# Modulation columns from stationary weights, and the second weight chunk in halves

## The chip, the cores and the metric

The kernel runs on one core of a Trainium2 chip. The metric is the device time of one execution in microseconds. The kernel before takes 1946.04 us, the median of three runs (1945.29 to 1946.46).

## The reference, cut to what matters

The program is one layer of a diffusion backbone over 1024 latent tokens and 256 context tokens, 1024 channels wide. It is written in float32:

```
mod_x = silu(c) @ w_mod + b_mod          # 6 * 1024 columns
mod_c = silu(c_ctx) @ w_mod + b_mod
sh1, sc1, g1, sh2, sc2, g2 = split(mod_x, 6);  csh1, csc1, ... = split(mod_c, 6)
hx = rms_norm(x, g) * (1 + sc1) + sh1
hc = rms_norm(ctx, g) * (1 + csc1) + csh1
fx, qx, kx, vx = split_projection(hx @ w_in)
fc, qc, kc, vc = split_projection(hc @ w_in)
# attention and a 2-D Fourier mixer over them, output projection,
# then a mixture of 16 experts (router, top 128 tokens for each expert) and a last norm
```

For this case only the beginning matters: the first 2048 columns of `silu(c) @ w_mod` and `silu(c_ctx) @ w_mod` (the shift `sh1` and the scale `sc1` for both streams), and the projection `h @ w_in`, whose `h` cannot be formed before shift and scale are known.

## The kernel before, in words

The kernel has three phases, one behind the other: `nc_phase_a` (modulation, norms, the input projection and the Fourier transform's first half), `nc_phase_b` (attention, output projection, router) and `nc_phase_m` (the experts). Each engine runs a list of its own, written out by hand in program order, and semaphores tie the lists together: `x.then_inc(s, 1)` counts up when an instruction is done, `wait_ge(s, n)` holds the engine's list until the count is reached. An engine never goes around a wait.

Float32 products are made in two ways. In the modulation, TensorE (called PE in the profile) multiplies plain float32 operands; each such product of the program shows as two instructions in the trace. In the projection, each operand is split into a rounded high part and a remainder (`w_hi`, `w_lo`, `h_hi`, `h_lo`), and three products hi*hi, hi*lo, lo*hi of 512 columns each replace one.

**Modulation columns.** The first 2048 columns of `w_mod` come as eight units of 256 columns, 1 MB each (L251), unit after unit on SyncE's (SP's) queue into eight slots of SBUF. Five of the units (`ON_PE`: 0, 1, 3, 4, 6) are multiplied by TensorE (L749): the two conditioning columns `c_sig` are the stationary operand (the weights loaded into the array), the unit's 256 columns move through, and the result is two rows of 256 in PSUM. ScalarE (ACT) copies each pair of rows to `c_rows` (L454), and when all five are there ten small transposes turn them into columns (L761). The other three units (`ON_DVE`: 2, 5, 7) are weighed and summed by VectorE (DVE, L575 and L576, 16 instructions a unit), and TensorE sums the result over the partitions by products with a vector of ones (L756), which gives columns at once. When all columns stand in bank 7 of PSUM (`c_col_done`), VectorE makes `mod_col` from them, six small instructions (L634 to L636, `cols_done`).

**The first latent tile.** ScalarE squares and scales the tile's rows (L369, L373; the root is on GpSimd, here POOL, `rstd`, L333 and L335), TensorE turns them (`turn`, L683), and ScalarE applies scale and shift to eight pieces of 128 columns (`turn` in its own list, L383), rounds them to `h_hi` (`high`, L389), and VectorE forms `h_lo` (`low`, L519). `turn(0, 0)` and `turn(0, 1)` are the lower and the upper four pieces.

**The weights.** `w_in` comes in three chunks of 512 columns, 2 MB each, in the order 1, 0, 2 behind the eight units on the same queue (L253). For each half of a chunk ScalarE rounds `w_raw` to `w_hi` (`weights`, L399) and VectorE forms `w_lo` (L515). `w_hi` of chunk 1 lies where units 0 and 1 lay, that of chunk 0 where units 2 and 3 lay; so the rounding also waits until those units are used.

**The projection** (`project`, from L687) then runs over ten tiles on TensorE, for each latent tile chunks 1, 0 and 2 with 24 products each (L699), with the turning of the next tile between them. `project(0, 1)` waits for `h_lo` of tile 0, for both halves of chunk 1 and for the rows' copies. VectorE's list beside it holds the remaining `w_lo`, the next `h_lo`, and the rest of the modulation (`modulation`, rows of `w_mod` through a ring of three buffers, which SP refills).

Of the kernel before, what the change touches and what calls it, by code (L numbers as in the profile page):

```python
# [143 lines left out]
def after(eng, sem_, v):  # L144

    if not (isinstance(v, int) and v <= 0):
        eng.wait_ge(sem_, v)


def nc_phase_a(nc, sem, a, psum, ident, ones, eps_c, ks, vs, x_odd, f_tok, q_d, mod_d, x_d, ctx_d, w_mod, w_in):  # L150
# [3 lines left out]
    def at(name, shape, dt, off):  # L154
# [45 lines left out]
    slot = [at(f"a_slot{i}", [P, KD, UM], F32, o * KB) for i, o in enumerate(slot_at)]  # L200

    s = {n: sem("a_" + n) for n in (
        "ident_done", "small_in", "kv_tab", "rope_in", "vec_t", "silu_done", "c_row_done", "c_col_done", "cols_done", "unit_used",
        "wh_done", "wl_done", "x_in", "ss_done", "mean_done", "rstd_done", "xn_done", "xT_done", "hf_done", "hh_done", "hl_done",
        "pj0", "pj1", "pj2", "ev0", "ev1", "ev2", "sq_done", "v_done", "g_done", "ss16_done", "eps_done", "rstd16_done", "rope_done",
        "qt_done", "qhi_done", "qlo_done", "q_out", "k_out", "mod_used", "row_mm", "row_ev", "row_out", "first_used",
        "dve_order", "pool_order", "wf_zero", "chan_in", "wf_in", "pm_done", "ab_mm", "ab_done", "g_mm", "gt_done", "mid_done", "q0_in")}
# [1 line left out]
    dft_in = [sem(f"f_dft_in{i}") for i in range(4)]  # L209
    unit_in = [sem(f"a_unit_in{i}") for i in range(8)]  # L210
    w_raw_in = [sem(f"a_w_raw_in{i}") for i in range(NCH)]
    ring_in = [sem(f"a_ring_in{i}") for i in range(RING)]
    NC_UNITS, NR_UNITS = 2 * D // UM, 4 * D // UM
    XT, PJ, QT, MB = 0, 2, 5, 7
# [20 lines left out]
    def w_parts(c):  # L235

        return 2 * (1, 0, 2).index(c)

    ON_DVE = (2, 5, 7)
    ON_PE = tuple(u for u in range(NC_UNITS) if u not in ON_DVE)  # L240

    with nc.Block() as block:

        @block.sync
        def _(sp):
# [4 lines left out]
            for u in range(NC_UNITS):  # L250
                sp.dma_start(slot[u][:, :, :].rearrange("p k n -> p (k n)"), w_mod[u]).then_inc(unit_in[u], 16)  # L251
            for c in (1, 0, 2):
                sp.dma_start(w_raw[:, c, :, :].rearrange("p k n -> p (k n)"), w_in[c]).then_inc(w_raw_in[c], 16)  # L253
                if c == 1:
                    sp.dma_start(g_qk[:, 0, :], a["q_norm_g"][0].partition_broadcast(P)).then_inc(s["kv_tab"], 16)
                    sp.dma_start(g_qk[:, 1, :], a["k_norm_g"][0].partition_broadcast(P)).then_inc(s["kv_tab"], 16)
# [61 lines left out]
        def _(pool):  # L318
# [11 lines left out]
            def rstd(n):  # L330
                st = stat[:, n % 2, :]
                pool.wait_ge(s["ss_done"], n + 1)
                pool.tensor_tensor(st[:, 1:2], st[:, 0:1], eps_c[:, 1:2], ALU.add).then_inc(s["mean_done"], 1)  # L333
                pool.wait_ge(s["mean_done"], n + 1)
                pool.tensor_tensor(st[:, 2:3], st[:, 1:2], eps_c[:, 0:1], ALU.pow).then_inc(s["rstd_done"], 1)  # L335
# [12 lines left out]
                pool.tensor_tensor(ss[:, 0, h0:NH], ss[:, 1, h0:NH], ss[:, 2, h0:NH], ALU.pow).then_inc(s["rstd16_done"], 1)  # L348

            rstd(0)  # L350
            rstd(1)
            for n in range(TS + 1):
                if 1 < n + 1 < TS:
# [6 lines left out]
        def _(act):  # L360
            def load_x(n):
                after(act, s["xT_done"], 2 * (n - 1))
                act.dma_start(xbuf(n)[:, :], x_d[n] if lat(n) else ctx_d[n - TL]).then_inc(x_in[n % 2], 16)
# [25 lines left out]
                act.activation(h_hi[n % 2][:, :, :], h_f[n % 2][:, :, :], ACT.Copy).then_inc(s["hh_done"], 1)  # L389

            def weights(c, half):
                act.wait_ge(w_raw_in[c], 16)
                if c == 1:
                    act.wait_ge(s["unit_used"], 2)
                elif c == 0:
                    act.wait_ge(s["unit_used"], 3)
                    act.wait_ge(s["first_used"], 1)
                k = slice(4 * half, 4 * half + 4)
                act.activation(w_hi[:, c, k, :], w_raw[:, c, k, :], ACT.Copy).then_inc(s["wh_done"], 1)  # L399

# [48 lines left out]
                           psum[:, 6, 0:2 * KD].rearrange("p (j k) -> p j k", k=KD), ACT.Silu).then_inc(s["silu_done"], 1)  # L449
            square(0)  # L450
            normal(0)
            for i, u in enumerate(ON_PE):
                act.wait_ge(s["unit_used"], i + 1)
                act.activation(c_rows[:, i * UM:(i + 1) * UM], psum[0:2, 2 + i % 2, 0:UM], ACT.Copy).then_inc(s["c_row_done"], 1)  # L454
                if i == 1:
                    load_x(2)
            weights(1, 0)
            weights(1, 1)
            turn(0, 0)
            turn(0, 1)  # L460
            high(0)
            square(1)
            normal(1)
# [36 lines left out]
        def _(dve):  # L500
# [130 lines left out]
            dve.wait_ge(s["c_col_done"], 1)  # L631
            cols = psum[:, 7, 0:4 * KD].rearrange("p (m k j) -> p m j k", k=KD, j=2)
            for j in range(2):
                dve.tensor_tensor(mod_col[:, 1, j, :], cols[:, 0, j, :], bg_col[:, 0:KD], ALU.add)  # L634
                link(dve.tensor_tensor(mod_col[:, 0, j, :], cols[:, 1, j, :], bg_col[:, KD:2 * KD], ALU.add))
                dve.scalar_tensor_tensor(out=mod_col[:, 0, j, :], in0=mod_col[:, 0, j, :], scalar=1.0,  # L636
                                         in1=g_col, op0=ALU.add, op1=ALU.mult).then_inc(s["cols_done"], 1)
            weights(1, 0)
            weights(1, 1)
            low(0)  # L640
            weights(0, 0)
# [31 lines left out]
        def _(pe):  # L673
# [12 lines left out]
            def project(n, c, part=range(KD)):  # L686
                if c == 2 and not lat(n) or c == 1:  # L687
                    pe.wait_ge(s["hl_done"], n + 1)
                if n == TS - 1:
                    pe.wait_ge(s["ev1"], TL)  # L690
                else:
                    after(pe, s[("ev0", "ev1", "v_done")[c]], n)
                if n == 0:
                    pe.wait_ge(s["wl_done"], w_parts(c) + 2)
                    if c == 1:
                        pe.wait_ge(s["c_row_done"], len(ON_PE))
                for k in part:
                    for x_, w_ in ((h_hi, w_hi), (h_hi, w_lo), (h_lo, w_hi)):
# [43 lines left out]
            for i, u in enumerate(ON_PE):  # L742
                if i == 1:
                    turn(0, 0)
                    turn(0, 1)
                pe.wait_ge(unit_in[u], 16)
                after(pe, s["c_row_done"], i - 1)
                for k in range(KD):
                    m = pe.matmul(psum[0:2, 2 + i % 2, 0:UM], c_sig[:, k, :], slot[u][:, k, :], start=(k == 0), stop=(k == KD - 1))  # L749
                m.then_inc(s["unit_used"], 1)  # L750
            for i, u in enumerate(ON_DVE):
                pe.wait_ge(s["first_used"], i + 1)
                for h in range(2):
                    for j in range(2):
                        b = 2 * u + h
                        pe.matmul(psum[:, 7, 2 * b + j:2 * b + j + 1], first_acc[i][:, j, h * P:(h + 1) * P], ones[:, 0:1], start=True, stop=True)  # L756
            pe.wait_ge(s["c_row_done"], len(ON_PE))
            for i, u in enumerate(ON_PE):
                for h in range(2):
                    b = 2 * u + h  # L760
                    m = pe.transpose(psum[:, 7, 2 * b:2 * b + 2], c_rows[:, (2 * i + h) * P:(2 * i + h + 1) * P], ident[0:2, 0:2])  # L761
            m.then_inc(s["c_col_done"], 1)
            for n in range(TS):
                if n == TL:
                    project(n, 2, range(KD // 4))
# [986 lines left out]
```

## Time and profile before

| | before |
|---|---|
| median of three runs | 1946.04 us |
| the profiled execution | 1948.3 us |
| its span, first to last instruction | 1946.5 us |
| PE busy | 1808.8 us (93%) |
| DVE busy | 1571.8 us (81%) |
| ACT busy | 1287.0 us (66%) |
| POOL busy | 352.1 us (18%) |
| mean granted TensorE clock | 0.974 |

The profile is that of one execution. Its times are counted from the first instruction. PE is busy nearly throughout; the modulation and the first projection lie in the first 58 us. PEld is TensorE's loading of stationary operands, which overlaps with its products. The granted clock is a share of TensorE's full 2.4 GHz, so 0.50 is 1.2 GHz.

### The profile page before, as it was taken

What the parts mean: (1) busy time and instruction counts of PE and PEld (TensorE: products, weight loads), DVE (VectorE), ACT (ScalarE), POOL (GpSimd) and SP (SyncE); (2) the same over time, 40 slices, a digit from 0 to 9 for tenths busy, and PEclk for the clock granted to TensorE, in tenths of its full rate; (3) what the DMA queues carried; (4) which work ended last, traced back from release to release, by engine and by line L of the source; (5) the groups of instructions that cost most, each with busy time, mean ns of one, the idle gap of its engine ahead of it and who ended that gap; (6) DMA issues with size and microseconds to landing.
All of it is one profiled execution on the core that took longest, in us unless ns stands there. A gap on an engine that the chain in (4) does not pass through costs nothing.

```text
span 1946.5 us, 27774 instructions
## 1 busy us (share of the span) xinstructions
PE 1808.8 (93%) x8627; PEld 1440.4 (74%) x8627; DVE 1571.8 (81%) x1944; ACT 1287.0 (66%) x1905; POOL 352.1 (18%) x319
## 2 busy tenths in 40 slices
PE   6999988999999997189999999999999999999995
PEld 3777766777777775178888888888888888888884
DVE  5888676777777774769998899999889989988986
ACT  3454375776677764167777777777777777777774
POOL 0333342222122222411011011101001100110113
PEclk8999999999999999589999999999999999999998
DMA  9465671221122201669999999999999999999996
GB/s 379 145 190 160 166 207 36 64 67 52 47 64 63 63 25 37 237 240 405 391 385 369 405 387 377 394 389 381 368 401 388 376 381 402 381 368 404 378 376 247
DMA packets 115204, 515.48 MB, mean 265 GB/s; under 512 B 17185, under 2 KB 43209, under 8 KB 64465
## 3 DMA queue, kind: packets, MB, share of 16 engines
q1 hardware_dynamic: 108960, 492.30, 67.6%
q0 software_dynamic: 4752, 17.30, 3.4%
q10 hardware_dynamic: 1440, 5.24, 0.7%
q8 instruction: 26, 0.43, 0.1%
q14 instruction: 26, 0.20, 0.0%
HBM read 484.86 MB, written 27.33 MB: 263 GB/s over the span
## 4 chain that ended last, share of the span: by engine, by line
PE 56%; DVE 2%; DMA 0%; POOL 0%; issue 0%; ACT 0%; DVEq 0%; ACTq 0%; POOLq 0%
PE banks L1688 36%; PE banks L1713 18%; PE banks L1700 1%; PE banks L1669 1%; DVE topi L1550 1%; DVE top L1548 1%; DVE cand L1551 1%; DVE raw L1643 0%; DMA xe<-h_scratch,icol 0%; POOL fst L1469 0%; DMA out<-raw 0%; ACT banks L1539 0%; DVE ysc L1610 0%; DVE ysc L1650 0%; POOL out L1473 0%
## 5 line engine op out<-in xcount | busy, mean ns | idle before, releaser
L1582 DVE TENSOR_TENSOR w_lo<-raw,w_hi 128x2048 fp32r<-128x2048 f32 x252 | 565.9, 2287 | 72.0 <-ACT w_hi L1491 72.0
L1491 ACT ACTIVATE w_hi<-raw 128x2048 fp32r<-128x2048 f32 x256 | 470.5, 1918 | 10.0 <-DMA raw<-in_w_exp 9.9
L1688 PE MATMUL banks<-w_hi,x_hi 128*128 128x512 f32 x1024 | 405.6, 396 | 1.4 <-DVE x_lo L1576 1.4
L1688 PE MATMUL banks<-w_hi,x_lo 128*128 128x512 f32 x1024 | 400.1, 391 | 0.0
L1688 PE MATMUL banks<-w_lo,x_hi 128*128 128x512 f32 x1024 | 399.7, 390 | 0.0
L1590 DVE TENSOR_TENSOR d_lo<-raw,d_hi 128x1024 fp32r<-128x1024 f32 x256 | 296.3, 1220 | 1.5 <-ACT d_hi L1513 1.4
L1513 ACT ACTIVATE d_hi<-raw 128x1024 fp32r<-128x1024 f32 x256 | 258.2, 1061 | 33.7 <-DMA raw<-in_w_exp 20.4
L1068 ACT ACTIVATE pth<-banks 128x384 fp32r<-128x384 f32 x320 | 157.2, 491 | 125.6 <-PE banks L1255 122.2
L1133 DVE TENSOR_TENSOR ptl<-banks,pth 128x384 fp32r<-128x384 f32 x320 | 177.7, 555 | 76.8 <-ACT pth L1068 72.0
L1688 PEld LDWEIGHTS banks<-w_hi,x_lo 128*128 128x128 f32 x1024 | 192.8, 188 | 40.8
L1688 PEld LDWEIGHTS banks<-w_hi,x_hi 128*128 128x128 f32 x1024 | 193.0, 188 | 39.7 <-DVE x_lo L1576 1.8
L1688 PEld LDWEIGHTS banks<-w_lo,x_hi 128*128 128x128 f32 x1024 | 193.1, 189 | 38.1
L1125 DVE TENSOR_REDUCE mn<-banks 128x1 f32<-128x512 f32 (+1 forms) x288 | 171.4, 595 | 56.4 <-PE banks L1238 55.8
L1422 POOL TENSOR_TENSOR carry<-carry 128x1 f32<-128x1 f32 x32 | 44.6, 1394 | 915.7 <-DVE ysc L1610 583.5
L1497 ACT ACTIVATE sil<-banks 128x512 f32<-128x512 f32 x64 | 38.2, 597 | 257.3 <-PE banks L1688 257.3
L1052 ACT ACTIVATE pr<-banks,mn 128x512 f32<-128x512 f32 (+1 forms) x288 | 176.6, 614 | 7.7 <-DVE mn L1129 7.2
L1255 PE MATMUL banks<-ident,pr 128*128 128x128 f32 x960 | 158.9, 275 | 10.8 <-DVE ptl L1133 9.0
L1237 PE MATMUL banks<-ks,qt 128*128 128x512 f32 (+1 forms) x288 | 144.3, 501 | 17.4 <-ACT pr L1052 15.9
L1713 PE MATMUL banks<-d_hi,h_hi 128*128 128x512 f32 x512 | 157.9, 390 | 2.6 <-DVE h_lo L1596 2.6
L1713 PE MATMUL banks<-d_hi,h_lo 128*128 128x512 f32 x512 | 157.7, 389 | 0.0
L1713 PE MATMUL banks<-d_lo,h_hi 128*128 128x512 f32 x512 | 157.7, 389 | 0.0
L1255 PEld LDWEIGHTS banks<-ident,pr 128*128 128x128 f32 x960 | 118.8, 140 | 46.3 <-DVE ptl L1133 16.8
(217 smaller groups left out, 2721.4 us busy)
## 6 DMA issues: line engine op xcount, KB each, us to landing
raw<-in_w_exp SPq DMA_DIRECT2D x384, 1024.0 KB, 7.7
a_ring<-in_w_mod SPq DMA_DIRECT2D x32, 512.0 KB, 7.3
qt<-q_scratch SPq DMA_DIRECT2D x64, 192.0 KB, 4.4
a_slot<-in_w_mod SPq DMA_DIRECT2D x8, 1024.0 KB, 13.9
a_w_raw<-in_w_in SPq DMA_DIRECT2D x3, 2048.0 KB, 28.7
q_scratch<-a_qst SPq DMA_DIRECT2D x16, 384.0 KB, 4.4
xr<-in_x SPq DMA_DIRECT2D x8, 512.0 KB, 5.1
acc_scratch<-x SPq DMA_DIRECT2D x8, 512.0 KB, 3.7
```

Source lines behind the costliest of these rows:

```text
L1052: act.activation(pr[(h // 3 % 2) * 3 + h % 3][:, lo:hi], psum[:, (NCH * h + c) % 4, 0:hi - lo], ACT.Exp, bias=mn[:, h, 3:4], scale=-1.0, a ...
L1068: act.activation(pth[:, k % 4, :], psum[:, PTB + k % 2, 0:REP * P], ACT.Copy).then_inc(s["hi_done"], 1)
L1125: ins = dve.tensor_reduce(mn[:, i, c:c + 1], psum[:, (NCH * i + c) % 4, 0:hi - lo], AX, ALU.min)
L1133: dve.tensor_tensor(ptl[:, k % 4, :], psum[:, PTB + k % 2, 0:REP * P], pth[:, k % 4, :].bitcast(F32), ALU.subtract).then_inc(s["lo_done"], 1)
L1237: pe.matmul(o, qt[:, i, 0, :], ks[:, i // 3, lo:hi], start=True, stop=False)
L1255: ins = pe.transpose(psum[:, PTB + k % 2, r * P:(r + 1) * P], pr[(g % 2) * 3 + r][:, kt * P:(kt + 1) * P], ident[:, :])
L1491: act.activation(w_hi[which][c][:, :], raw[which][c][:, :], ACT.Copy).then_inc(s["hi_done"], 1)
L1513: act.activation(d_hi[k][:, :], raw[2][k // 2][:, k % 2 * D:(k % 2 + 1) * D], ACT.Copy).then_inc(s["d_hi_done"], 1)
L1582: dve.tensor_tensor(w_lo[which][c][:, :], raw[which][c][:, :], w_hi[which][c][:, :].bitcast(F32), ALU.subtract).then_inc(s["lo_done"], 1)
L1590: dve.tensor_tensor(d_lo[k][:, :], raw[2][k // 2][:, k % 2 * D:(k % 2 + 1) * D], d_hi[k][:, :].bitcast(F32), ALU.subtract).then_inc(s["d_l ...
L1688: i = pe.matmul(psum[:, 2 * (j % 2) + which, :], x_[par][:, k, :], w_, start=(k == 0 and w_ is hi and x_ is x_hi), stop=(k == KD - 1 and x ...
L1713: i = pe.matmul(psum[:, Y + h, :], x_[:, k, :], w_[k][:, h * 512:(h + 1) * 512], start=(j == 0 and k == 0 and x_ is h_hi and w_ is d_hi), ...
```

## The change

The units on TensorE become 0, 2, 3, 5 and 7, those on VectorE 1, 4 and 6. For a unit on TensorE the weights are now the stationary operand: for each half of 128 columns and each of eight pieces of the contraction, 128 x 128 of the unit are loaded and the two columns of `c_sig` move through; the result is two columns in bank 7. The rows, their copies and their transposes are gone. The order on TensorE is otherwise kept: unit 0, the turning of tile 0, the other units, the products with ones.

Chunk 1 of `w_in` comes in two transfers, and ScalarE rounds its lower half when the first has landed. `w_lo` of the lower half goes to GpSimd, between `rstd(0)` and `rstd(1)`; VectorE makes only the upper half. The upper half of tile 0's scale and shift (`turn(0, 1)`) goes from ScalarE to VectorE, ahead of its `weights(1, 1)`. `project(0, .)` waits for the halves of `w_lo` one by one. Between the columns and `project(0, 1)` TensorE runs 14 products of 512 columns into a bank that `project(0, 1)` overwrites; they wait for the first half of `w_hi`.

```diff
-    ON_DVE = (2, 5, 7)
+    ON_DVE = (1, 4, 6)
 # SP
-                sp.dma_start(w_raw[:, c, :, :].rearrange("p k n -> p (k n)"), w_in[c]).then_inc(w_raw_in[c], 16)
+                if c == 1:
+                    for half in range(2):
+                        sp.dma_start(w_raw[:, c, 4 * half:4 * half + 4, :].rearrange("p k n -> p (k n)"),
+                                     w_in[c][:, 4 * half * UC:(4 * half + 4) * UC]).then_inc(w_raw_in[c] if half else w_half_in, 16)
+                else:
+                    sp.dma_start(w_raw[:, c, :, :].rearrange("p k n -> p (k n)"), w_in[c]).then_inc(w_raw_in[c], 16)
 # GpSimd
             rstd(0)
+            pool.wait_ge(s["rstd_done"], 1)
+            pool.wait_ge(s["wh_done"], 1)
+            pool.tensor_tensor(w_lo[:, 1, 0:4, :], w_raw[:, 1, 0:4, :], w_hi[:, 1, 0:4, :].bitcast(F32), ALU.subtract).then_inc(s["wl0_done"], 1)
+            pool.wait_ge(s["wl0_done"], 1)
             rstd(1)
 # ScalarE
             def weights(c, half):
-                act.wait_ge(w_raw_in[c], 16)
+                act.wait_ge(w_half_in if c == 1 and half == 0 else w_raw_in[c], 16)
                 if c == 1:
-                    act.wait_ge(s["unit_used"], 2)
+                    act.wait_ge(s["unit_used"], 1)
+                    act.wait_ge(s["first_used"], 1)
...
-            for i, u in enumerate(ON_PE):
-                act.wait_ge(s["unit_used"], i + 1)
-                act.activation(c_rows[:, i * UM:(i + 1) * UM], psum[0:2, 2 + i % 2, 0:UM], ACT.Copy).then_inc(s["c_row_done"], 1)
-                if i == 1:
-                    load_x(2)
+            load_x(2)
             weights(1, 0)
             weights(1, 1)
             turn(0, 0)
-            turn(0, 1)
             high(0)
 # VectorE
-            weights(1, 0)
+            dve.wait_ge(s["xT_done"], 2)
+            dve.wait_ge(s["cols_done"], 2)
+            for k in range(4, 8):
+                ins = dve.tensor_scalar(h_f[0][:, k, :], psum[:, XT + 1, k % 4 * P:(k % 4 + 1) * P],
+                                        mod_col[:, 0, 0, k:k + 1], mod_col[:, 1, 0, k:k + 1], ALU.mult, ALU.add)
+            ins.then_inc(s["hf_done"], 1)
             weights(1, 1)
             low(0)
 # TensorE
-                after(pe, s["c_row_done"], i - 1)
-                for k in range(KD):
-                    m = pe.matmul(psum[0:2, 2 + i % 2, 0:UM], c_sig[:, k, :], slot[u][:, k, :], start=(k == 0), stop=(k == KD - 1))
+                for h in range(2):
+                    b = 2 * u + h
+                    for k in range(KD):
+                        m = pe.matmul(psum[:, 7, 2 * b:2 * b + 2], slot[u][:, k, h * P:(h + 1) * P], c_sig[:, k, :], start=(k == 0), stop=(k == KD - 1))
...
-            pe.wait_ge(s["c_row_done"], len(ON_PE))
-            for i, u in enumerate(ON_PE):
-                for h in range(2):
-                    b = 2 * u + h
-                    m = pe.transpose(psum[:, 7, 2 * b:2 * b + 2], c_rows[:, (2 * i + h) * P:(2 * i + h + 1) * P], ident[0:2, 0:2])
-            m.then_inc(s["c_col_done"], 1)
+            pe.wait_ge(s["wh_done"], 1)
+            for i in range(14):
+                pe.matmul(psum[:, PJ + 1, :], w_hi[:, 1, 0, 0:P], w_hi[:, 1, 0, :], start=True, stop=True)
```

## Rows read from the trace of the kernel before

**Rows 1.** The page's chain that ended last, shares by engine and line:

```profile
PE 56%; DVE 2%; DMA 0%; POOL 0%; issue 0%; ACT 0%; DVEq 0%; ACTq 0%; POOLq 0%
```

**Rows 2.** Stretches: length, busy and count of PE, PEld, DVE, ACT, POOL; clock; DMA:

```profile
31.70:33.90 2.20, 0.00 (x0) 0.00 (x0) 2.20 (x6) 0.26 (x1) 0.00 (x0) 0.98 0.96 382
37.00:43.40 6.40, 0.00 (x0) 0.00 (x0) 6.26 (x9) 5.35 (x12) 0.39 (x1) 0.50 0.98 413
43.40:47.40 4.00, 3.99 (x9) 3.14 (x10) 0.35 (x1) 3.33 (x3) 0.55 (x2) 0.50 1.00 373
47.50:50.90 3.40, 3.40 (x17) 2.77 (x16) 3.40 (x2) 3.40 (x3) 0.00 (x0) 1.00 0.07 28
```

**Rows 3.** Waits of PE from 40 to 260 us: total, times, longest:

```profile
PE banks L712 <- DVE a_qkn L560: 6.4, 7, 1.3
```

**Rows 4.** Timeline to 52 us: start, busy, instruction, idle before and its releaser:

```profile
9.20 5.64 PE L749 MATMUL banks<-a_slot,a_c_sig 128*2 128x256 f32 x16 [2.95 <-DMA a_slot<-in_w_mod]
14.66 5.63 DVE L576 SCALAR_TENSOR_TENSOR a_first<-a_slot,a_c_sig,a_first 128x256 f32<-128x256 f32 x14
15.80 13.97 PE L749 MATMUL banks<-a_slot,a_c_sig 128*2 128x256 f32 x64
21.50 0.62 DVE L575 TENSOR_SCALAR a_first<-a_slot,a_c_sig 128x256 f32<-128x256 f32 x2 [1.22 <-DMA a_slot<-in_w_mod]
29.71 1.95 PE L756 MATMUL banks<-ones,a_first 128*128 128x1 f32 x16
33.65 3.71 ACT L399 ACTIVATE a_w_hi<-a_w_raw 128x2048 fp32r<-128x2048 f32 x2 [3.46 <-DMA a_w_raw<-in_w_in]
33.96 1.87 PE L756 MATMUL banks<-ones,a_first 128*128 128x1 f32 x8 [2.31 <-DVE a_first L576]
37.02 0.17 DVE L634 TENSOR_TENSOR a_mod_col<-banks,a_bg_col 128x8 f32<-128x8 f32 x1 [3.12 <-PE banks L761]
37.73 4.49 DVE L515 TENSOR_TENSOR a_w_lo<-a_w_raw,a_w_hi 128x2048 fp32r<-128x2048 f32 x2
37.91 2.90 ACT L383 ACTIVATE a_h_f<-banks,a_mod_col 128x128 f32<-128x128 f32 x8 [0.56 <-DVE a_mod_col L636]
40.84 1.06 ACT L389 ACTIVATE a_h_hi<-a_h_f 128x1024 fp32r<-128x1024 f32 x1
42.14 1.22 DVE L519 TENSOR_TENSOR a_h_lo<-a_h_f,a_h_hi 128x1024 fp32r<-128x1024 f32 x1
43.41 0.79 PE L699 MATMUL banks<-a_w_hi,a_h_hi 128*128 128x512 f32 x1 [6.42 <-DVE a_h_lo L519]
51.60 0.19 PEld L699 LDWEIGHTS banks<-a_w_hi,a_h_hi 128*128 128x128 f32 x1 [0.38 <-DVE a_w_lo L515]
```

**Rows 5.** The eight units' transfers: issues with first and last start, time to landing:

```profile
L251 SPq DMA_DIRECT2D a_slot<-in_w_mod x8: 360/440/738, 2.2 to 6.3; - x8
DMA to landing us min/median/max: 6.8/13.9/21.4
```

**Rows 6.** The timeline's operations nearest to those that the change adds:

```profile
64.05 4.01 POOL L341 TENSOR_TENSOR a_sq<-a_prj 128x1024 f32<-128x1024 f32 x1 [1.55 <-ACT vs L420]
84.15 2.74 POOL L341 TENSOR_TENSOR a_sq<-a_prj 128x1024 f32<-128x1024 f32 x1 [1.01 <-DVE a_qkn L560]
105.60 0.42 DVE L523 TENSOR_TENSOR vs<-banks,vs 128x256 fp32r<-128x256 f32 x1
```

**Rows 7.** GpSimd's own subtractions of this shape, ns min/median/max:

```profile
L1411 POOL TENSOR_TENSOR w_lo<-raw,w_hi x4: 4524/4526/4537, 797.7 to 811.2; 128x2048 fp32r<-128x2048 f32 x4
```

**Rows 8.** Later stretches of TensorE at the low clock, columns as in the stretches above:

```profile
303.47:306.88 3.41, 3.41 (x14) 2.95 (x13) 1.14 (x3) 0.95 (x3) 0.00 (x0) 0.50 0.00 0
306.90:309.00 2.10, 2.10 (x11) 1.49 (x10) 1.42 (x4) 0.97 (x4) 0.00 (x0) 1.00 0.04 1
781.31:784.72 3.41, 2.67 (x13) 2.68 (x14) 0.00 (x0) 0.62 (x2) 0.68 (x1) 0.50 0.38 154
```

**Rows 9.** The timeline's products of the router, sixteen columns moving:

```profile
782.95 3.43 PE L1221 MATMUL banks<-wrt,h2t 128*128 128x16 f32 x16
```

More of the change, by code:

```diff
@@ L202, in nc_phase_a @@
     s = {n: sem("a_" + n) for n in (
-        "ident_done", "small_in", "kv_tab", "rope_in", "vec_t", "silu_done", "c_row_done", "c_col_done", "cols_done", "unit_used",
-        "wh_done", "wl_done", "x_in", "ss_done", "mean_done", "rstd_done", "xn_done", "xT_done", "hf_done", "hh_done", "hl_done",
+        "ident_done", "small_in", "kv_tab", "rope_in", "vec_t", "silu_done", "c_col_done", "cols_done", "unit_used",
+        "wh_done", "wl_done", "wl0_done", "x_in", "ss_done", "mean_done", "rstd_done", "xn_done", "xT_done", "hf_done", "hh_done", "hl_done",
         "pj0", "pj1", "pj2", "ev0", "ev1", "ev2", "sq_done", "v_done", "g_done", "ss16_done", "eps_done", "rstd16_done", "rope_done",
@@ L211, in nc_phase_a @@
     w_raw_in = [sem(f"a_w_raw_in{i}") for i in range(NCH)]
+    w_half_in = sem("a_w_half_in")
     ring_in = [sem(f"a_ring_in{i}") for i in range(RING)]
@@ L391, in weights @@
             def weights(c, half):
-                act.wait_ge(w_raw_in[c], 16)
+                act.wait_ge(w_half_in if c == 1 and half == 0 else w_raw_in[c], 16)
                 if c == 1:
-                    act.wait_ge(s["unit_used"], 2)
+                    act.wait_ge(s["unit_used"], 1)
+                    act.wait_ge(s["first_used"], 1)
                 elif c == 0:
                     act.wait_ge(s["unit_used"], 3)
-                    act.wait_ge(s["first_used"], 1)
                 k = slice(4 * half, 4 * half + 4)
@@ L630, in _ @@
                 first_unit(i, u)
-            dve.wait_ge(s["c_col_done"], 1)
+            dve.wait_ge(s["c_col_done"], len(ON_DVE))
             cols = psum[:, 7, 0:4 * KD].rearrange("p (m k j) -> p m j k", k=KD, j=2)
@@ L692, in project @@
                     after(pe, s[("ev0", "ev1", "v_done")[c]], n)
-                if n == 0:
-                    pe.wait_ge(s["wl_done"], w_parts(c) + 2)
-                    if c == 1:
-                        pe.wait_ge(s["c_row_done"], len(ON_PE))
                 for k in part:
+                    if n == 0 and k % 4 == 0:
+                        if c == 1 and k == 0:
+                            pe.wait_ge(s["wl0_done"], 1)
+                        else:
+                            pe.wait_ge(s["wl_done"], w_parts(c) + k // 4)
                     for x_, w_ in ((h_hi, w_hi), (h_hi, w_lo), (h_lo, w_hi)):
@@ L755, in _ @@
                         b = 2 * u + h
-                        pe.matmul(psum[:, 7, 2 * b + j:2 * b + j + 1], first_acc[i][:, j, h * P:(h + 1) * P], ones[:, 0:1], start=True, stop=True)
-            pe.wait_ge(s["c_row_done"], len(ON_PE))
-            for i, u in enumerate(ON_PE):
-                for h in range(2):
-                    b = 2 * u + h
-                    m = pe.transpose(psum[:, 7, 2 * b:2 * b + 2], c_rows[:, (2 * i + h) * P:(2 * i + h + 1) * P], ident[0:2, 0:2])
-            m.then_inc(s["c_col_done"], 1)
+                        m = pe.matmul(psum[:, 7, 2 * b + j:2 * b + j + 1], first_acc[i][:, j, h * P:(h + 1) * P], ones[:, 0:1], start=True, stop=True)
+                m.then_inc(s["c_col_done"], 1)
+            pe.wait_ge(s["wh_done"], 1)
+            for i in range(14):
+                pe.matmul(psum[:, PJ + 1, :], w_hi[:, 1, 0, 0:P], w_hi[:, 1, 0, :], start=True, stop=True)
             for n in range(TS):
```

## The prediction

> **What bounds the kernel now.** I read the page's chain first: TensorE holds 56% of the span in the chain that ended last [rows 1], and everything behind the first projection hangs on TensorE's order. So the question is by how much the first projection moves, and whether what follows moves with it. The stretches come next: between 37.0 and 43.4 us TensorE does nothing, while VectorE (6.26 us) and ScalarE (5.35 us) are nearly full [rows 2]. The timeline says what it waits for [rows 4]. `project(0, 1)` starts at 43.41, released by `h_lo`. Backwards: `h_lo` 1.22 us from 42.14, held up by the two `w_lo` (4.49 us from 37.73); `h_hi` 1.06; eight pieces of scale and shift 2.90 from 37.91; the columns, whose first small instruction starts at 37.02 and whose six take 0.8 us; before them the products with ones (1.87 us from 33.96), released by VectorE's third unit, and the ten transposes. In parallel the weights land, 33.65, and ScalarE rounds both halves until 37.4. So two arms meet: columns and weights. Last, the projection runs low at first: nine products in 4.0 us at a granted clock of 0.50 (1.2 GHz), then some fifteen whole ones in 3.4 us at 1.00 (2.4 GHz), 0.44 against 0.227 us each [rows 2]. That costs 9 x 0.21 = 1.9 us.
>
> **The weights' arm.** The last unit has landed by 6.3 + 21.4 = 27.7 us [rows 5], chunk 1 by 33.65. Halfway between is 30.7: there the first half lands. ScalarE rounds it until 32.6 (half of 3.71 is 1.86), then, waiting for the second, until 35.5 [rows 4]. The extra issue on SP costs nothing as long as the queue is ahead of the transfers (the units were all issued by 6.3 us). `load_x(2)` is issued on ScalarE some 3 us earlier, no longer behind two copies; its 0.5 MB shares the transfers with the units and delays some of them by up to 0.5/1 of the 2.46 us that a 1 MB unit takes ((21.50 - 9.20)/5), 1.2 us, but not chunk 1, as the bytes ahead of that are the same.
>
> GpSimd's half of `w_lo`: no such operation stands in this stage, but the same shape later takes 4.52 to 4.54 us [rows 7]. So 32.6 + 4.5 = 37.1. A square on GpSimd takes 4.01 us in one place and 2.74 in another [rows 6]; with that ratio it would be 6.6 us, ready at 39.2. I take 4.5, a row of the operation itself; either end is before `h_lo` (below), so it costs nothing. Behind it in GpSimd's list waits `rstd(1)`, for which `normal(1)` and behind it the remaining roundings wait on ScalarE; ScalarE reaches `square(1)` only at 38.1, so with 4.5 us nobody waits, with 6.6 us 1 us is lost there, which the 5.4 us of `project(0, 1)` mostly cover.
>
> **The columns' arm on VectorE.** One unit takes 0.62 + 5.63 = 6.2 us [rows 4]. Units 1, 4 and 6 land at about 11.7, 19 to 20 and 24 to 25. So it ends at 17.9, 26 and 32.3 (33.9 before).
>
> **The columns' arm on TensorE** is the disputed term. A unit was 8 products, 16 in the trace; 64 of them took 13.97 us, 3.5 us a unit at the high level [rows 4]. Now it is 16 products, 32 in the trace, each with a load of 128 x 128 and two columns. The nearest row is the products with ones, same load and one column: 16 in 1.95 us, 0.122 each, and, when the clock was down, 8 in 1.87, 0.234 each [rows 4]. So a unit costs 3.9 us at the high level or 7.5 at the low one, against 3.5 before; the change pays here and wins only the copies and the ten transposes (1.2 us).
>
> Which level? Before, 16 products of 5.64 us and those behind them at 0.218 say that the first ten or so ran at the low pace, for 4.3 us. If the new stream lifts the clock as fast: 18 instructions in 4.3 us, the other 14 in 1.7, unit 0 done at 15.2; turning 1.0; then nothing waits but unit 7, with 3.9 us each: 20.1, 24.0, 27.9, 31.8. All 24 products with ones then take 2.9, the last eight behind VectorE's 32.3: columns at 34.7, `mod_col` at 35.5 instead of 37.8. That is just when ScalarE has rounded the weights.
>
> For the high level: a stretch of 3.41 us in which loads filled 2.95 us ended with the clock up [rows 8]; the units make TensorE busy without a gap for 22 us, and each long unbroken stretch here ends at the high level. Against: 2.67 busy us of transposes and 16-column products [rows 8, 9] did not lift it, though not all of that stretch was busy; and it had dropped to 0.98 on average by 33.9, only 2.2 us after the narrow products ended [rows 2]. The router's sixteen then ran evenly at 0.214 each. The Trainium skill ("TensorE: Matmul & The Clock Gate", Part 4: PE-mode transpose) says that transposes don't count as busy for the clock in the way other products do; carried over to this stream, TensorE would stay at 1.2 GHz. The trace has a mixed stretch that rose and a narrow one that didn't, so it leaves this open; by that rule the sum is that of rival B. I give the high level the better chance, 2 in 3.
>
> **From there to the projection.** ScalarE: four pieces 1.45 us from 35.5 (half of 2.90), `h_hi` 1.06, at 38.1. VectorE: its four pieces from 35.5. Such a piece from PSUM on VectorE is not in the trace; a PSUM operand of 256 columns takes 0.42 [rows 6], so at most 0.42, at least half of it, 0.21; I take 0.25 (near the width), 1.0 in all: 36.5. `w_lo`'s upper half 2.25 (half of 4.49): 38.75. `h_lo` 1.22: 40.0. The projection starts at 40.0 rather than 43.4: **-3.4 us** (-3.0 if the pieces cost 0.42 and the columns come 0.2 late, -4.0 if VectorE is free by the time `h_hi` is). Nothing behind VectorE's new wait is hurt: its list holds only `w_lo` and `h_lo`, which need the same columns.
>
> The 14 wide products start at 34.7 and end by 37.9 at the high pace, by 40.9 at the low one. They add no result. If the clock outlasts the 2.1 us to 40.0, the 1.9 us of the slow start are gone; if not, they are paid again. I take three quarters: **-1.5 us** (0 to -1.9).
>
> `project(0, 0)` waited 0.38 us for `w_lo` [rows 4]. ScalarE gets to chunk 0 some 3.5 us earlier and VectorE as well, so I count that wait as nearly gone: **-0.3** (0 to -0.4). In sum -5.2 us. From then on TensorE is short of nothing but VectorE's rotated queries, 6.4 us in 7 waits [rows 3], and these follow TensorE's own products. So the shift reaches the end.
>
> The profiled execution took 1948.3 us, its span 1946.5; the sum of differences goes against the median of the runs, 1946.04: **1940.8 us**.
>
> **Rivals.** A (the forecast), chance 0.58: 1939.0 to 1943.0, from the ends above (-7 to -3).
>
> B, slower, 0.32: the clock stays at 1.2 GHz while weights are stationary. Five units at 7.5 us and eight transposes at twice the pace (2.0): 9.2 + 37.5 + 2.0 = 48.7; products with ones 24 x 0.234 = 5.6: columns at 54.3 (with the router's 0.214 a unit is 6.8 and they stand at 50). Then the wide products, up to 14 x 0.44 = 6, now on the path, less once the clock rises: start at 55.5 to 60 instead of 43.4, less 1.9 for a warm start and 0.4: +10 to +14, **1958 us**. It decides as soon as the columns come later than about 40 us, a mean of some 4.6 us a unit. For it speak the router's products and the drop at 33.9, against it the stretch that rose.
>
> C, no change, 0.10: VectorE is nearly as late as TensorE in each tile [rows 3], and if its part is paced by the ring's transfers rather than by TensorE, the start is given back there over eight tiles: all but 1 us, 1945. Against it speaks that no single wait is above 1.3 us.
>
> **How the numbers follow.** About 0.2% (3.9 us) is what a measurement of this kernel can tell from no change. A falls beyond it in 4 of 5 cases: faster 0.46. Same: 0.12 of A and 0.10 of C, 0.22. Slower: B, 0.32. The time is A's. As A and C hold less than 8 in 10 with their edges, the range reaches over B's middle: 1939 to 1959; A's own is 1939 to 1943.
>
> **What would show it.** In the changed profile: the pace of the new unit products, 0.12 us (A) or 0.21 to 0.23 (B), and the granted clock at 35 us; the first small column instruction at about 34.7; the first rounding at 30.7; GpSimd's subtraction of 4.5 us done at 37; the projection's start at 40.0 and whether its first nine products take 2 or 4 us; PE's waits for rotated queries still near 6.4 us. The prediction is wrong if the columns are later than 38, or if the projection starts by 41 and the end doesn't move by 3.

## The result, and the profile after

The changed kernel takes 1962.40 us, the median of six runs (1959.92 to 1964.22), against 1946.29 for the kernel before in the same comparison: a ratio of 1.0075, 95% interval 1.0060 to 1.0089 (the two medians alone would give 1.0083). It is slower, and its time lies above the range I gave. The profiled execution took 1963.47 us with a span of 1961.7, 15.2 us more than before.

The chain of the page looks as it did [rows 1]:

```profile
PE 55%; DVE 2%; DMA 0%; POOL 0%; issue 0%; ACT 0%; DVEq 0%; ACTq 0%; POOLq 0%
```

TensorE's order carries the span as before, so a later start of the projection can move the end. The timeline of the changed kernel, with the columns of [rows 4]:

```profile
9.53 6.96 PE L761 MATMUL banks<-a_c_sig,a_slot 128*128 128x2 f32 x32 [3.27 <-DMA a_slot<-in_w_mod]
18.10 27.30 PE L761 MATMUL banks<-a_c_sig,a_slot 128*128 128x2 f32 x128
31.19 1.91 ACT L409 ACTIVATE a_w_hi<-a_w_raw 128x2048 fp32r<-128x2048 f32 x1 [21.49 <-DMA a_w_raw<-in_w_in]
33.25 4.53 POOL L359 TENSOR_TENSOR a_w_lo<-a_w_raw,a_w_hi 128x2048 fp32r<-128x2048 f32 x1 [24.73 <-ACT a_w_hi L409]
45.26 5.26 PE L768 MATMUL banks<-ones,a_first 128*128 128x1 f32 x24
50.38 5.90 PE L773 MATMUL banks<-a_w_hi 128*128 128x512 f32 x14
50.56 0.17 DVE L639 TENSOR_TENSOR a_mod_col<-banks,a_bg_col 128x8 f32<-128x8 f32 x1 [18.92 <-PE banks L768]
51.46 1.37 DVE L646 TENSOR_SCALAR a_h_f<-banks,a_mod_col 128x128 f32<-128x128 f32 x4
56.21 0.50 PE L710 MATMUL banks<-a_w_hi,a_h_hi 128*128 128x512 f32 x1
62.21 0.50 PE L710 MATMUL banks<-a_w_hi,a_h_hi 128*128 128x512 f32 x1
```

The units on TensorE (L761) take 6.96 us for 32 instructions and 27.30 for 128: 0.213 to 0.218 us each, the pace that I had read as the low level's (0.21 to 0.23), from the first to the last. VectorE waits 18.92 us for the columns. The columns stand at 50.56 instead of 37.02, `project(0, 1)` starts at 56.21 instead of 43.41 (+12.8), and since it runs at full pace from its first product, `project(0, 0)` starts 10.6 us late (62.21 against 51.60). Where the units are meant, "a product" below is one such instruction of the trace; two of them make one product of the program.

The remaining 4.6 us of the 15.2 come in the tiles. PE's waits there and VectorE's, from 50 to 260 us, and VectorE's in the kernel before, from 40 to 260 us, columns as in [rows 3]:

```profile
PE banks L723 <- DVE a_qkn L565: 8.1, 6, 2.2
DVE a_acc L581 <- DMA a_ring<-in_w_mod: 27.8, 8, 5.6
```

```profile
DVE a_acc L576 <- DMA a_ring<-in_w_mod: 26.6, 7, 4.7
```

TensorE waits 8.1 us for rotated queries instead of 6.4, and behind two of these waits, at 158 and at 223 us, its granted clock falls to 0.50 for some 3.4 us, which in the kernel before it doesn't do in the tiles. In this stretch (columns as in [rows 2]) the clock is 0.66 on average:

```profile
157.00:162.00 5.00, 4.71 (x18) 3.76 (x18) 5.00 (x10) 1.16 (x2) 2.75 (x1) 0.66 0.07 16
```

### The profile page after: what moved, and what is told of

It is laid out like the page before. It is cut to its first block, busy times and chain, and to the rows that moved or that the text cites. A ratio compares the mean times of both kernels' runs of the same rounds, so it can differ in the third digit from the quotient of the medians.

```text
span 1961.7 us, 27938 instructions
## 1 busy us (share of the span) xinstructions
PE 1830.7 (93%) x8711; PEld 1473.4 (75%) x8711; DVE 1571.2 (80%) x1947; ACT 1284.3 (65%) x1896; POOL 370.8 (19%) x320
## 4 chain that ended last, share of the span: by engine, by line
PE 55%; DVE 2%; DMA 0%; POOL 0%; issue 0%; ACT 0%; DVEq 0%; ACTq 0%; POOLq 0%
PE banks L1699 36%; PE banks L1724 17%; PE banks L1711 1%; PE banks L1680 1%; DVE topi L1561 1%; DVE top L1559 1%; DVE cand L1562 1%; DVE raw L1654 0%; DMA xe<-h_scratch,icol 0%; POOL fst L1480 0%; DMA out<-raw 0%; ACT banks L1550 0%; POOL fst L1478 0%; DVE ysc L1621 0%; DVE ysc L1661 0%
## 5 line engine op out<-in xcount | busy, mean ns | idle before, releaser
L1433 POOL TENSOR_TENSOR carry<-carry 128x1 f32<-128x1 f32 x32 | 68.5, 2140 | 905.8 <-DVE ysc L1621 583.6
L1136 DVE TENSOR_REDUCE mn<-banks 128x1 f32<-128x512 f32 (+1 forms) x288 | 171.5, 596 | 56.1 <-PE banks L1249 55.6
L1508 ACT ACTIVATE sil<-banks 128x512 f32<-128x512 f32 x64 | 38.4, 599 | 265.1 <-PE banks L1699 265.1
```

The source lines that it names most:

```text
L1136: ins = dve.tensor_reduce(mn[:, i, c:c + 1], psum[:, (NCH * i + c) % 4, 0:hi - lo], AX, ALU.min)
```

## The experiments

Unless said otherwise, an edit is made to the changed kernel; "..." stands for code left out. The ratios are to the kernel before, which had medians of 1947.85, 1947.48 and 1947.25 us in the three comparisons.

### Is it the two moving columns?

Each product moves 128 columns, the two of `c_sig` repeated 64 times:

```diff
-    m = pe.matmul(psum[:, 7, 2 * b:2 * b + 2], slot[u][:, k, h * P:(h + 1) * P], c_sig[:, k, :], ...)
+    m = pe.matmul(psum[:, 7, 2 * b:2 * b + P], slot[u][:, k, h * P:(h + 1) * P],
+                  c_sig[:, k, :].unsqueeze(1).broadcast_to([P, P // 2, 2]), ...)
```

> The changed kernel with one edit: each unit product moves 128 columns (the two conditioning columns, repeated 64 times) past the same stationary weights; the 126 extra columns land on places of the bank that later products overwrite. Theory 1: the clock stayed at 1.2 GHz because almost nothing moved through the array while weights were loaded. Then this stream lifts it some 4 us in: the pace falls from 0.213 to 0.12 to 0.14 us, columns at 34 to 36 us instead of 50.6, the first projection at 40, the time about 1941 us, as rival A and the forecast had it. Theory 2: the loads are slow in this stage for another reason (transfers into SBUF and VectorE's reads beside them), whatever the clock. Then the pace stays at 0.21, and the time at 1960 to 1964 us or more.

1950.67 us, ratio 1.0010 (1.0001 to 1.0019). Its timeline:

```profile
8.86 6.17 PE L761 MATMUL banks<-a_c_sig,a_slot 128*128 128x128 f32 x32 [2.37 <-DMA a_slot<-in_w_mod]
15.74 10.88 PE L761 MATMUL banks<-a_c_sig,a_slot 128*128 128x128 f32 x96
33.17 4.57 POOL L359 TENSOR_TENSOR a_w_lo<-a_w_raw,a_w_hi 128x2048 fp32r<-128x2048 f32 x1 [24.43 <-ACT a_w_hi L409]
35.10 0.17 DVE L639 TENSOR_TENSOR a_mod_col<-banks,a_bg_col 128x8 f32<-128x8 f32 x1 [2.80 <-PE banks L768]
35.38 2.39 DVE L641 SCALAR_TENSOR_TENSOR a_mod_col<-a_mod_col,a_bg_col 128x8 f32<-128x8 f32 x1
42.99 0.79 PE L710 MATMUL banks<-a_w_hi,a_h_hi 128*128 128x512 f32 x1 [4.60 <-DVE a_h_lo L524]
```

With 64 times the moving columns a product takes 0.113 us (10.88 / 96) instead of 0.213, and the columns stand at 35.10, where I had forecast 34.7. So the number of moving columns made the columns late; that it did so by the clock, the next run shows. But the win that I forecast behind it doesn't come. L641, an instruction of 8 columns that takes 0.17 us elsewhere, takes 2.39 and ends at 37.77, when GpSimd's subtraction ends (33.17 + 4.57 = 37.74); I call this the hold. And the 14 wide products are done by 38.4, TensorE has nothing for 4.6 us, and the projection's first products run at a granted clock of 0.50 again.

### Does the narrow stream hold a clock that is up?

Twenty products of the identity run ahead of unit 0, and their results aren't used:

```diff
+            for i in range(10):
+                pe.matmul(psum[:, 5, 0:P], ident[:, :], ident[:, :], start=True, stop=True)
             pe.wait_ge(s["small_in"], 16 * 4)
             pe.transpose(psum[:, 6, 0:5 * KD], vec[:, :], ident[0:5 * KD, 0:5 * KD]).then_inc(s["vec_t"], 1)
+            for i in range(10):
+                pe.matmul(psum[:, 5, 0:P], ident[:, :], ident[:, :], start=True, stop=True)
             pe.wait_ge(s["silu_done"], 1)
```

> The changed kernel with 20 products of 128 columns (identity by identity, results unused) ahead of unit 0, so that the clock can be up when the unit stream begins. Theory 1: the first unit products run at 0.12 us, and some microseconds later the pace falls back to 0.213 for the rest of the stream, because the stream does not hold the clock; columns at about 46 to 49 us. Theory 2: 0.21 from the first product on. Theory 3 (the stream only lacks a start: it holds the clock once it is up): 0.12 throughout, columns near 34.

1962.82 us, one run. Its units in the timeline, and two stretches of them:

```profile
9.42 3.63 PE L765 MATMUL banks<-a_c_sig,a_slot 128*128 128x2 f32 x32
13.98 27.09 PE L765 MATMUL banks<-a_c_sig,a_slot 128*128 128x2 f32 x128
```

```profile
9.40:13.00 3.60, 3.60 (x35) 3.60 (x34) 1.45 (x5) 0.75 (x1) 0.00 (x0) 1.00 1.01 426
16.00:41.00 25.00, 25.00 (x119) 25.00 (x119) 13.93 (x37) 3.82 (x2) 4.52 (x1) 0.50 1.02 423
```

Warmed, unit 0 runs at 0.113 us a product and a clock of 1.00; with the engine still busy without a gap the clock then falls, and units 2 to 7 run at 0.50 for 25 us. So this stream of weight loads with two columns neither lifted the clock (in the changed kernel) nor held it (here), though TensorE's busy share is 100%. The columns stand at 46.22 and the projection starts at 52.09, 4.1 us earlier than in the changed kernel; this one run is no faster, as its tiles take 22.06 us each and those of the changed kernel 21.13 (measured as in the loop below).

### What is the rest of the change worth?

This run has the old units (`c_sig` stationary, rows, copies, transposes, VectorE on 2, 5 and 7) with all the rest of the change:

```diff
-    ON_DVE = (1, 4, 6)
+    ON_DVE = (2, 5, 7)
...
-                for h in range(2):
-                    b = 2 * u + h
-                    for k in range(KD):
-                        m = pe.matmul(psum[:, 7, 2 * b:2 * b + 2], slot[u][:, k, h * P:(h + 1) * P], c_sig[:, k, :], ...)
+                for k in range(KD):
+                    m = pe.matmul(psum[0:2, 2 + i % 2, 0:UM], c_sig[:, k, :], slot[u][:, k, :], ...)
```

> The changed kernel with the units computed as before the change (two rows of 256, copies, ten transposes, VectorE's units 2, 5 and 7), all other parts kept: the halves of chunk 1, GpSimd's share, VectorE's four pieces, the 14 wide products. It tells what these parts are worth by themselves. Theory 1 (all the loss is in the units): faster than before, columns at 37 as before, first projection at about 42.5 and at full clock: 1943 to 1945 us. If GpSimd's share or the second transfer were part of the loss, it would be above 1947 us.

1946.24 us, ratio 0.9993 (0.9983 to 1.0004): no gain that can be told, where I had expected 1943 to 1945. The hold is there as well:

```profile
33.60 4.54 POOL L359 TENSOR_TENSOR a_w_lo<-a_w_raw,a_w_hi 128x2048 fp32r<-128x2048 f32 x1 [24.73 <-ACT a_w_hi L409]
35.70 2.46 DVE L645 SCALAR_TENSOR_TENSOR a_mod_col<-a_mod_col,a_bg_col 128x8 f32<-128x8 f32 x1
43.38 0.50 PE L714 MATMUL banks<-a_w_hi,a_h_hi 128*128 128x512 f32 x1 [3.00 <-DVE a_h_lo L528]
```

The columns stand at 35.4, but VectorE's first small instruction with both operands in SBUF takes 2.46 us, until GpSimd is done at 38.14, and the projection starts where it did before, at 43.38. The Trainium skill ("GPSIMD Engine Reference", section 8, Key points) says that GpSimd shares its SBUF interfaces with VectorE and that instructions with two SBUF inputs contend there; both traces agree, and put the price at 2.2 to 2.3 us for one small instruction.

The changed kernel without the 14 wide products:

```diff
-            for i in range(14):
-                pe.matmul(psum[:, PJ + 1, :], w_hi[:, 1, 0, 0:P], w_hi[:, 1, 0, :], start=True, stop=True)
```

> The changed kernel without the 14 wide products. If they held up the first projection, it starts earlier than 56.2 by up to 4 us and the time falls below 1960. If they only ran beside the scale, the shift and the remainder, the projection still starts at about 56.2, but its first nine or so products run at 0.43 instead of 0.23: 1 to 2 us slower than the changed kernel, about 1964 us.

1963.56 us, ratio 1.0079 (1.0066 to 1.0092). `project(0, 1)` starts at 56.17, as with the wide products, and its first 13 products take 0.43 us each, up to 61.9. So the wide products lie beside VectorE's work and save some 2.5 us at the start; the end shows 1.2 us of it, less than the medians tell apart.

### Without GpSimd's share

This is the kernel with 128 moving columns, in which VectorE makes the low half of `w_lo` itself, ahead of its wait for the columns:

```diff
-            pool.tensor_tensor(w_lo[:, 1, 0:4, :], w_raw[:, 1, 0:4, :], w_hi[:, 1, 0:4, :].bitcast(F32), ALU.subtract)...
+            weights(1, 0)          # VectorE
             dve.wait_ge(s["c_col_done"], len(ON_DVE))
```

> The wide-moving kernel (unit products with 128 moving columns) with GpSimd's subtraction given back to VectorE, which makes the low half of the first weight piece itself ahead of its wait for the columns. Theory 'hold': GpSimd's 4.57 us subtraction held VectorE's small instruction on the scale column (2.39 us for 0.17) until it ended; without it that instruction takes 0.17 us, the columns stand by 37, h_lo is made by 41 and the first projection starts at 41.0 (42.99 with the share). The cost of the move is VectorE's 2.3 us, mostly beside the wait for the columns: at most 0.6 us. Rival 'VectorE's own': the 2.39 us came from something else (a queue, a semaphore, the operand itself), stays, and the first projection starts at 43 or later, since VectorE now has 2.3 us more to do. Time by the first theory 1945 to 1949, by the rival 1951 or more.

With 26 wide products in place of 14:

> The same, with 26 wide products in place of 14 after the columns, so that TensorE is busy until the first projection (12 more at 0.21 us each, 2.6 us: from 38.4 to 41.0). Theory 'idle gap': the fall of the clock at 41.9 in the wide-moving kernel came from TensorE's 4.6 us without work behind the 14 products; with the gap filled, the first 11 products of the projection take 0.21 and not 0.43 us, and project(0, 0) ends at 47 to 48 (51.26 with the gap, 51.6 before the change). Rival: the clock falls for another reason (the load of the stretch before), and the first products are slow all the same; then 50 or later. Time 1942 to 1946 by the first if the tiles keep the lead, 1947 to 1950 by the rival. A third outcome, project(0, 0) early and the end not, says that the tiles give the lead back.

With 22, and `low(0)` ahead of `weights(1, 1)` on VectorE:

> As the one with 26 wide products, with 22, and VectorE makes h_lo ahead of the low half 4 to 7 of the weights, which the first projection needs only 12 products in. h_lo then waits for ScalarE's high part (39.0) alone and stands at 40.2: the first projection starts at 40.3 instead of 41.0, 0.7 us earlier, and the low half is there at 42.5, before the 13th product at 42.9. Rival: the order doesn't matter, because ScalarE's high part is later than I take it to be. Time: 0.7 us under the kernel with 26, within what can be told apart only if the tiles keep the lead.

The old units, VectorE making the low half:

> The kernel with the old units (the modulation vector moving over the weights... that is, stationary) and the rest of the change, with GpSimd's subtraction given back to VectorE as well: what the change is worth without both of its costly parts. Theory 'hold': VectorE's instruction on the scale column takes 0.17 and not 2.46 us, and the first projection starts at 41 (43.38 with the share, 43.41 before the change); the time is 1 to 2 us under the 1946.2 of the kernel with the share if the tiles keep the lead, and no change if they give it back. Rival 'VectorE's own': 2.46 us stay, start 43.4 or later.

| kernel | us | ratio | `project(0, 1)` starts |
|---|---|---|---|
| 128 columns, no share of GpSimd | 1947.06 | 0.9994 (0.9985 to 1.0003) | 41.20 |
| the same, 26 wide products | 1948.18 | 0.9996 (0.9985 to 1.0008) | 44.21 |
| 22 wide products, `h_lo` first | 1948.85 | 1.0004 (0.9996 to 1.0013) | 41.07 |
| old units, no share of GpSimd | 1944.58 | 0.9983 (0.9973 to 0.9994) | 43.03 |

The hold is gone in all four; in the first one's timeline the instruction of 2.39 us is back at 0.17, and the projection starts at 41.2, at full pace:

```profile
35.53 0.17 DVE L638 SCALAR_TENSOR_TENSOR a_mod_col<-a_mod_col,a_bg_col 128x8 f32<-128x8 f32 x1
41.20 0.39 PE L704 MATMUL banks<-a_w_hi,a_h_hi 128*128 128x512 f32 x1
```

That also removes the reason for more wide products: here the clock had fallen to 0.50 by 35, during the products with ones (one moving column), and was up again by 41.2 behind 14 of them. 26 of them, half at the low pace, last until 44.4 and push the projection back: a miss. So is the order of `h_lo`: there the 22 products, not `h_lo`, end at 41.1. The old units' start is a miss by 2 us: VectorE's third unit was done at 34.4 and not 33.6, and the last products and transposes behind it took longer, so that the columns came at 37.4.

The main miss is the time. The first and third kernel have 4.6 and 4.2 us of lead at tile 0 (GpSimd's first square at 59.49 and 59.88; 64.05 before, [rows 6]) and, by the medians, nothing at the end. The profiled execution of the first, 1951.96 us, is its slowest; that of the third, 1946.32, is one of its fastest and still has 2.9 us of the lead at tile 7. Where does the lead go?

### The loop in the tiles

One turn in the trace of the changed kernel (SPq is SP's issuing of transfers):

```profile
136.83 1.29 DVE L572 TENSOR_TENSOR a_qst<-banks,a_qst 128x512 fp32r<-128x512 f32 x2
138.15 3.50 SPq L282 DMA_DIRECT2D ks<-a_qst  x4
141.70 1.29 SPq L285 DMA_DIRECT2D q_scratch<-a_qst  x2
143.03 9.62 SPq L272 DMA_DIRECT2D a_ring<-in_w_mod  x4
150.59 1.67 DVE L581 SCALAR_TENSOR_TENSOR a_acc<-a_ring,a_c_sig,a_acc 128x256 f32<-128x256 f32 x4 [5.56 <-DMA a_ring<-in_w_mod]
156.01 1.22 DVE L565 TENSOR_TENSOR a_qkn<-a_qkn,a_sq 128x1024 f32<-128x1024 f32 x1
```

The split queries (136.83) are stored by six transfers, the load of the modulation's next quarter is issued behind them (143.03), VectorE waits 5.56 us for it, then rotates (156.01), and TensorE's next queries wait for that: a closed loop through SP's queue. A turn takes 20.67 us on average in the kernel before and 20.9 to 22 in those without GpSimd's share. The move:

```diff
-                if n >= 2:
-                    store(n - 2)
                 if n < TL:
                     load(4 * n + 3)
+                if n >= 2:
+                    store(n - 2)
```

It was made in the kernel before, in the changed kernel, in the one with the old units and no share of GpSimd, and in the one with 22 wide products:

> The kernel before the change with one thing moved: in each tile's turn on the transfer queue, the load of the fourth quarter of the modulation rows is issued ahead of the stores of the queries and keys of two tiles earlier, not behind them. It tests why a lead at the start of the tiles isn't kept. Theory 'loop': each tile turns in a loop (queries on TensorE, their split on VectorE, six stores on the transfer queue, then the quarter's load, its landing 7 us later, VectorE's 4 to 5 us wait for it, rotation, next queries), as long as TensorE's own work or longer, so that TensorE waits 0.5 to 1.3 us per tile (6.4 us in all) and the kernel gains what the loop loses: the stores take 4 us of issue (148.45 to 152.7), the quarter before is used by 151.1, so the load goes out 1.7 to 2 us earlier, TensorE's waits for the rotated queries fall to near nothing, and phase A ends 5 to 8 us earlier: 1939 to 1943. Rival 'TensorE-bound': the waits are slack that comes back elsewhere, time within 2 us of before.

> The changed kernel with the same move. It asks where the 4.6 us come from that the changed kernel loses in the tiles beside the 10.6 us it loses ahead of them. Theory 'loop': they are longer turns of the loop (waits of 8.1 us for rotated queries and two stretches of low clock behind them); with the load ahead of the stores both kernels lose the waits, and the difference to the kernel before with the same move is 10 to 12 us, not 16. Rival: the 4.6 us belong to the change itself (for instance x rows or stores arriving in another order), and the difference stays at 15 to 17 us.

> The kernel with the old units and VectorE making its own low half (1944.6), with the same move: its first projection leads by the 0.4 us start and full pace, 2.6 us at the first tile's squares. By 'loop' it keeps that lead and wins 5 to 8 us more: 1936 to 1941, under the kernel before with the move by 2 to 3. By 'TensorE-bound' it stays at 1943 to 1946.

> The kernel with units of 128 moving columns, 22 wide products and h_lo first (1948.8, although its first tile's squares lead by 4.2 us), with the same move. By 'loop' the lead of 4.2 us is kept and the time is 1 to 2 us under the kernel with the old units and the same move: 1935 to 1940. By a rival 'warm units' the 128 moving columns cost something later that no view names yet, and it stays 2 us or more above the kernel with the old units.

The time of a tile is the distance between GpSimd's squares of the tiles 1 and 7, by 6:

| kernel | us | ratio | a tile without the move | with it |
|---|---|---|---|---|
| before | 1938.36 | 0.9954 (0.9936 to 0.9972) | 20.67 | 19.34 |
| changed | 1951.91 | 1.0018 (1.0006 to 1.0030) | 21.13 | 19.34 |
| old units, no share of GpSimd | 1934.90 | 0.9931 (0.9912 to 0.9950) | 20.94 | 19.34 |
| 22 wide products, `h_lo` first | 1938.83 | 0.9949 (0.9931 to 0.9968) | 20.88 | 19.34 |

In the kernel before with the move, SP issues the load ahead of the stores, VectorE waits 0.27 us for it, and TensorE waits once for rotated queries, where it waited seven times [rows 3]; timeline, then PE's and VectorE's waits from 40 to 260 us, then a stretch of 100 us in the tiles, first in the kernel before and then with the move:

```profile
148.58 0.37 SPq L266 DMA_DIRECT2D a_ring<-in_w_mod  x1
149.01 2.58 SPq L276 DMA_DIRECT2D ks<-a_qst  x4
153.12 1.67 DVE L576 SCALAR_TENSOR_TENSOR a_acc<-a_ring,a_c_sig,a_acc 128x256 f32<-128x256 f32 x4 [0.27 <-DMA a_ring<-in_w_mod]
```

```profile
PE banks L712 <- DVE a_qkn L560: 0.5, 1, 0.5
DVE a_acc L576 <- DMA a_ring<-in_w_mod: 2.2, 6, 0.7
```

```profile
100.00:200.00 100.00, 94.82 (x435) 73.03 (x434) 78.82 (x136) 44.37 (x94) 38.57 (x25) 1.00 0.63 174
```

```profile
100.00:200.00 100.00, 100.00 (x466) 77.89 (x464) 83.62 (x142) 48.58 (x105) 38.19 (x27) 1.00 0.69 196
```

All four now take the same 19.34 us a tile, and TensorE, busy for 94.82 of 100 us before, is busy for all 100: it sets the pace, and a lead or a lag at tile 0 is kept through the tiles. Against the kernel before with the move, the one with the old units leads by 3.3 us at the first square and by 3.2 at tile 7, the last one by 3.8 at both. The changed kernel is behind by 9.65 us at the first square (73.93 against 64.28) and by 10.29 at tile 7 (210.65 against 200.36). The two profiled executions differ by 11.0 us (1952.25 and 1941.22); the medians by 13.5, more than the 10 to 12 expected and less than the rival's 15. So the loop made most of the 4.6 us by the profiled executions (15.2 us became 11.0), and about half by the medians (16.1 became 13.5). Where the 2 us between the medians lie is not shown. A candidate is the wait for the output weights, of which more below: 5.9 us in the changed kernel with the move, 3.4 in the kernel before with it.

The last kernel is a miss: 1938.83, where I expected it under the one with the old units, which has 1934.90; the number is that of the rival "warm units". At the end of the tiles they are 1 us apart. Then TensorE waits for the output weights, which GpSimd scales in attention's beginning; the waits of the old units' kernel and of the last one, there:

```profile
289.53 1.13 PE L1217 MATMUL banks<-wout,mix 128*128 128x512 f32 x2 [0.46 <-POOL wout L1035]
```

```profile
292.55 2.07 PE L1209 MATMUL banks<-wout,mix 128*128 128x512 f32 x2 [5.58 <-POOL wout L1027]
```

5.58 against 0.46 us: ahead of that chain GpSimd waited 17.9 us for a transfer (the gain of the later norm) rather than 15.2. Why the transfer came later was not tried. It lands 12.0 to 12.6 us after its issue in six of the fourteen traces and 14.5 to 15.6 in eight. The kernel before, which has no unit of 128 columns, is among the late ones (15.0), but so are all five kernels that have them, so the rival isn't ruled out.

The kernel with the old units, without GpSimd's share and with the load ahead of the stores, at 1934.90 us, is the fastest measured here.

## Why the prediction was wrong

**The failed step is the columns' arm on TensorE**, "I give the high level the better chance, 2 in 3". It was the low pace throughout: 0.213 us a product, some 7 us a unit, where I had bounded it by 7.5 and taken 3.9. I weighed an unbroken busy stretch [rows 8] as what lifts the clock; the narrow kernel is busy without a gap for 27 us and stays low, the warmed one falls while busy, and 128 moving columns alone restore 0.113. The rows of the router [rows 9], sixteen columns and no rise, were the nearer ones in kind: few columns behind a full weight load. The Trainium skill ("TensorE: Matmul & The Clock Gate", Part 4: PE-mode transpose) says of transposes that they don't count as busy for the clock as other products do; carried over to this stream it gave rival B's sum. The trace agrees in effect, with 0.213 us a product throughout; no run shows that the reason is the same as for transposes.

**Rival B's mechanism held**: the units at the router's pace put the columns at 50 (measured 50.56) and the start at 55.5 to 60 (56.21). Its time, 1958, missed 1962.4 by the tiles' part.

**The step "So the shift reaches the end" failed as well.** I read TensorE's 6.4 us of waits [rows 3] as following its own products. They follow a loop over SP's queue, which was my rival C; its mechanism is real, for with 128 moving columns a lead of 4.2 to 4.6 us is gone in the medians, and the tiles shorten to 19.34 us once the load goes first. A lag does reach the end, and grew from 10.6 to 15.2 us on the way. So forecast A would not have reached 1940.8 even with a stream at full pace: the kernels that come nearest to it have 1947.06 to 1948.85.

**GpSimd's half "costs nothing"** was right for the time at which it is done (37.78, forecast 37.1) and wrong in the forecast's own case: with the columns at 35 it holds VectorE until then, and the start is 43.0 to 43.4, not 40.0. In the changed kernel it is done 12.8 us before the columns, and costs nothing there. I had also read the two squares of [rows 6] as one instruction at two speeds; the last section has what they show.

**Right by their rows:** the first rounding (31.19, forecast 30.7); VectorE's units, done at 31.6 (32.3); columns to projection 5.65 us (5.3), its four pieces 1.37 (1.0, at most 1.7); the slow start gone, worth some 2.5 us where the wide products run out just before the projection; and the wait in front of `project(0, 0)` gone. One sum is off: the ends that I name for A (4.0, 1.9 and 0.4) add up to 6.3, not 7.

## What to carry to other kernels

Before making the large operand the stationary one, time the stream with two moving columns and with many: here two ran at 0.213 us a product through 27 us without a gap, 128 at 0.113, and a busy share of 100% told nothing of it. Before giving GpSimd a share, look which two-operand SBUF instructions VectorE has on the path in that time. And before counting on a lead, ask whether the waits in the loop behind it follow the engine's own work or a queue; one load moved ahead of six stores was worth 9 us here, more than any part of the change gained.

## What was not expected of the hardware

A product of the trace with a full float32 weight load (half a product of the program) takes 0.113 us with 2 and with 128 moving columns, when the clock is up; the further 126 columns cost nothing here. And the granted clock stands at 1.00 in the changed kernel's rows up to 56 us although the pace is the low one: the trace's first record of the clock, a rise to 1.00, stands at 55.6 us (in the warmed kernel at 7.6), and ahead of it the duration of the instructions is the evidence.

GpSimd's subtraction didn't slow VectorE's small instruction but held it to its own end (2.39 and 2.46 us for 0.17), while those with an operand in PSUM beside it took their 0.17 us. It goes the other way too. GpSimd's square takes 1.89 us in the kernel before with the move, where VectorE has no instruction with two operands in SBUF beside it; the second square of [rows 6] starts in the middle of one:

```profile
103.75 1.89 POOL L341 TENSOR_TENSOR a_sq<-a_prj 128x1024 f32<-128x1024 f32 x1 [0.84 <-ACT vs L420]
```

```profile
62.26 4.04 DVE L576 SCALAR_TENSOR_TENSOR a_acc<-a_ring,a_c_sig,a_acc 128x256 f32<-128x256 f32 x10
83.92 1.22 DVE L519 TENSOR_TENSOR a_h_lo<-a_h_f,a_h_hi 128x1024 fp32r<-128x1024 f32 x1
```

From VectorE's end, 85.14, another 1.89 us is 87.0, and the square ends at 84.15 + 2.74 = 86.9; the first one starts during ten sums that end at 66.30, and 66.30 + 1.89 is 68.2 against its end at 68.1. So 2.74 and 4.01 us are the same 1.89 with a wait in front, to within 0.15 us. Not every GpSimd instruction holds VectorE: beside the root of 16 columns (3.02 us from 151.82 in the kernel before with the move) the four sums at 153.12 shown above took 1.67 us as elsewhere.
